# Where two input projections stand in a two-layer decoder step: at the gate and in the router instead of ahead of the output projection

## The reference

```python
for i in range(DEPTH):                                   # DEPTH = 2
    mix, nb, ns = mixer(rms_norm(x, norm_mix_g[i]), ...) # ends in m @ w_o
    x = x + mix
    hn = rms_norm(x, norm_ffn_g[i])
    if i % 2 == 0: f = swiglu(hn, w_dense_gu, w_dense_down)      # layer 0
    else:          f = moe(hn, w_router, w_gu, w_down)           # layer 1
    x = x + f
    gate = jax.nn.sigmoid(rms_norm(x, norm_ple_g[i]) @ w_ple_gate[i])
    x = x + gate * (p[i] @ w_ple[i])                     # the layer-input projection

def moe(h, ...):                                         # 8 experts, 2 per token
    logits = h @ w_router
    top_v, top_i = lax.top_k(logits, 2)
    top_w = jax.nn.softmax(top_v, axis=-1)
    ...
```

## Time and profile before

| | |
|---|---|
| median of three runs | 1804.52 us (1803.7 to 1807.8) |
| the profiled execution's own time | 1805.45 us |
| its span, first to last instruction | 1803.7 us |
| TensorE busy | 1756.8 us, 97% |
| VectorE / ScalarE / GpSimd busy | 1431.7 / 1079.1 / 151.7 us |
| mean granted TensorE clock | 0.99 of 2.4 GHz |

### The profile page before, as it was taken

One profiled execution on the slowest core, in us unless ns is written; L12 is line 12 of the kernel. 1 busy time (PEld: TensorE's weight loads), 2 busy tenths in 40 slices (PEclk: granted clock), 3 DMA queues, 4 the chain that ended last, 5 costly groups with the idle time before them and its releaser, 6 DMA issues.

```text
span 1803.7 us, 27952 instructions
## 1 busy us (share of the span) xinstructions
PE 1756.8 (97%) x10593; PEld 1562.5 (87%) x10593; DVE 1431.7 (79%) x1326; ACT 1079.1 (60%) x894; POOL 151.7 (8%) x158
## 2 busy tenths in 40 slices
PE   7999999999989999899999999999999999999996
PEld 6999999999989999788888888888888888888876
DVE  5875676566678766598898998998988989889886
ACT  4335544334443455476777777776777777777763
POOL 2112210000331113100000000000000000000003
PEclk9999999999999999899999999999999999999999
DMA  9754555655555545299999999999999999999970
GB/s 270 243 179 155 172 175 166 194 177 166 186 186 169 174 155 169 89 367 376 328 360 342 357 356 335 363 365 330 357 361 339 355 364 336 362 343 347 366 271 25
DMA packets 278010, 483.74 MB, mean 268 GB/s; under 512 B 7918, under 2 KB 126910, under 8 KB 277938
## 3 DMA queue, kind: packets, MB, share of 16 engines
q1 hardware_dynamic: 274734, 472.67, 75.3%
q0 software_dynamic: 2992, 9.92, 2.0%
q10 hardware_dynamic: 212, 0.14, 0.0%
HBM read 476.83 MB, written 5.87 MB: 268 GB/s over the span
## 4 chain that ended last, share of the span: by engine, by line
PE 90%; DVE 4%; DMA 2%; ACT 2%; issue 1%; POOL 0%; SPq 0%; DVEq 0%; POOLq 0%; ACTq 0%
PE PS L1656 11%; PE PS L1660 11%; PE PS L1659 11%; PE PS L1845 10%; PE PS L1848 10%; PE PS L1849 10%; PE PS L1676 6%; PE PS L1679 6%; PE PS L1680 6%; DMA raw<-in_w_in 2%; DVE wlo L1319 2%; PE PS L1636 1%; ACT whi L834 1%; PE PS L1694 1%; PE PS L2050 1%
## 5 line engine op out<-in xcount | busy, mean ns | idle before, releaser
L1319 DVE TENSOR_TENSOR wlo<-raw,whi 128x2048 fp32r<-128x2048 f32 x450 | 1036.9, 2307 | 241.9 <-ACT whi L834 237.6
L834 ACT ACTIVATE whi<-raw 128x2048 fp32r<-128x2048 f32 x450 | 862.3, 1918 | 393.4 <-PE PS L1845 166.9
L1656 PE MATMUL PS<-whi,xh 128*128 128x512 f32 x896 | 353.5, 395 | 1.0 <-DVE wlo L1319 0.9
L1660 PE MATMUL PS<-whi,xl 128*128 128x512 f32 x896 | 350.2, 391 | 0.0
L1659 PE MATMUL PS<-wlo,xh 128*128 128x512 f32 x896 | 349.4, 390 | 0.0
L1845 PE MATMUL PS<-xh,whi 128*128 128x264 f32 x1184 | 341.3, 288 | 6.2 <-DVE pg__51 L1361 3.8
L1848 PE MATMUL PS<-xl,whi 128*128 128x264 f32 x1184 | 337.9, 285 | 0.0
L1849 PE MATMUL PS<-xh,wlo 128*128 128x264 f32 x1184 | 337.8, 285 | 0.0
L1845 PEld LDWEIGHTS PS<-xh,whi 128*128 128x128 f32 x1184 | 225.5, 190 | 7.3 <-issue 4.0
L1848 PEld LDWEIGHTS PS<-xl,whi 128*128 128x128 f32 x1184 | 225.5, 190 | 0.2
L1849 PEld LDWEIGHTS PS<-xh,wlo 128*128 128x128 f32 x1184 | 224.3, 189 | 0.0
(11 more groups left out here) (291 smaller groups left out, 1841.9 us busy)
## 6 DMA issues: line engine op xcount, KB each, us to landing
raw<-in_w_exp_gu SPq DMA_DIRECT2D x224, 1024.0 KB, 5.8
raw<-in_w_exp_down SPq DMA_DIRECT2D x112, 1024.0 KB, 5.6
raw<-in_w_in SPq DMA_DIRECT2D x44, 1024.0 KB, 5.2
raw<-in_w_dense_gu SPq DMA_DIRECT2D x28, 1024.0 KB, 5.0
raw<-in_w_dense_down SPq DMA_DIRECT2D x16, 896.0 KB, 5.1
raw<-in_w_o SPq DMA_DIRECT2D x8, 1024.0 KB, 4.9
raw<-in_w_ple_gate SPq DMA_DIRECT2D x8, 1024.0 KB, 6.0
scr<-in_state_ret POOLq DMA_DIRECT2D x8, 512.0 KB, 4.8
```

The source lines that it names most:

```text
L834: nc.scalar.activation(whi[:, c % CAST, :], raw[:, c % RAW, :], ACT.Copy).then_inc(hi_done, 1)
L1319: v.tensor_tensor(wlo[:, c % CAST, :], raw[:, c % RAW, :], whi[:, c % CAST, :].bitcast(F32), ALU.subtract).then_inc(lo_done, 1)
L1656: ins = mm(PS[:, bank, :], gh[:, 128 * kk:128 * kk + 128], wh, start=kk == 0, stop=False)
L1660: ins = mm(PS[:, bank, :], gl[:, 128 * kk:128 * kk + 128], wh, start=False, stop=kk == 7)
```

## The change

Four things are changed together.

1. `pw` leaves its place between `ret` and `o` in both layers; `o` now starts with `chunk_late`, on the operands of `m_lo`.
2. In layer 0, `pw` stands between the down-projection and the gate, with the norm's sum of squares behind its tile 4. ScalarE copies tiles 0 to 4, takes the root, copies 5 to 7; VectorE makes the reciprocal first and then casts gate chunks 1 and 2.
3. In layer 1, `pw` stands in the router, tile by tile: tile 0 ahead of everything, 1 and 2 around the logits, 3 ahead of the ranks, 4 ahead of the gather, 5 between gather and turning, 6 and 7 behind the turning. It uses two of the ring's banks. The token groups are reordered, the low ones in three banks. The router weights are split in layer 1's `o` loop.
4. Experts are picked on the logits as they come, without the token's norm factor, which is positive and so changes no order; the factor is multiplied into the difference of the two picked logits before the exponential. Root, reciprocal and Newton step come behind the selection. The counts go to bank 7 and are ready together with the ranks; the gating block comes behind the copy of the first gather.

The core of the diff:

```diff
-        for name, n in (("in", 14), ("conv", 2), ("gate", 8), ("ret", 2), ("pw", 1), ("o", 4)):
+        order = [("in", 14), ("conv", 2), ("gate", 8), ("ret", 2), ("o", 4)]
+        order += [("ffn", 44), ("pw", 1), ("pg", 4)] if l == 0 else [("pw", 1), ("ffn", 0), ("pg", 4)]
+        for name, n in order:
...
@@ the mixer's end, TensorE
-                pw_pe(chunk, l)
-                for i in range(4):
-                    chunk(b["o"] + i, t["o"] + 2 * i, 8, 2, frt[:, 8:16, :], frt[:, 16:24, :],
-                          each=(m_lo, [8 * l + k + 1 for k in range(8)]) if i == 0 else None)
+                chunk_late(b["o"], t["o"], (m_lo, [8 * l + k + 1 for k in range(8)]), None, frt[:, 8:16, :], frt[:, 16:24, :])
+                for i in range(1, 4):
+                    chunk(b["o"] + i, t["o"] + 2 * i, 8, 2, frt[:, 8:16, :], frt[:, 16:24, :])
...
+                    pw_pe(chunk, l)
                     ple_pe(pe, chunk, stat, 0)
...
-            chunk(b["pw"], t["pw"], 2, 8, ph[:, 2 * l:2 * l + 2, :], pl[:, 2 * l:2 * l + 2, :])
+            chunk(b["pw"], t["pw"], 2, 8, ph[:, 2 * l:2 * l + 2, :], pl[:, 2 * l:2 * l + 2, :], norm=2, at_tile=4)
@@ layer 0's gate, ScalarE
                     dense_act(act, cast, root, split_x)
+                    act.wait_ge(tile_taken, t["pw"])
+                    for j in range(5):
+                        take_pw(j)
+                    root(NORM_OF["ple", 0])
+                    for j in range(5, KT):
+                        take_pw(j)
+                    cast(b["pw"] + AHEAD)
                     ple_act(act, cast, root, split_x, 0)
@@ layer 0's gate, VectorE
                     dense_dve(dve, v, cast, recip, take, split_x)
+                    recip(NORM_OF["ple", 0])
+                    cast(b["pw"] + AHEAD)
+                    dve.wait_ge(tile_taken, t["pg"])
                     ple_dve(dve, v, cast, recip, take, split_x, 0)
@@ the router, TensorE
+            def pw_tile(j):
+                if j == 0:
+                    ready(PWC)
+                pe.wait_ge(tile_taken, PW1 - 2 + j if j < 2 else PW1 + j - 1)
+                for k in range(2):
+                    ...
+                ins.then_inc(tile_ready, 1)
...
+            pw_tile(0)
+            token_hi(0)
+            token_hi(1)
+            pe.wait_ge(xl_ready, 32 + 4)
+            token_lo(0)
+            token_lo(1)
+            token_lo(2)
+            pw_tile(1)
+            token_hi(2)
             pe.wait_ge(wr_lo, 1)
...
             ins.then_inc(lgT_ready, 1)
+            token_hi(3)
+            pw_tile(2)
             pe.wait_ge(lgT_done, 1)
...
+            token_lo(3)
+            token_lo(4)
+            token_hi(4)
+            token_hi(5)
+            token_lo(5)
+            pw_tile(3)
+            pe.wait_ge(route_act, 1)
+            pe.wait_ge(route_dve, 1)
...
+            ins.then_inc(rank_ready, 1)
+            pw_tile(4)
...
             gather(0)
+            pw_tile(5)
             turn_operands(0)
+            pw_tile(6)
+            pw_tile(7)
             pe.wait_ge(routed, 1)
@@ the router, VectorE
-            dve.wait_ge(route_act, 1)
-            v.memset(rg[:, :, 1:2], 0.0).then_inc(dve_chain, 1)
-            n_chain[0] += 1
-            link(v.tensor_scalar(rt[:, 232:235], PS[0:TT, 7, 24:27], 1.0 / D, EPS, ALU.mult, ALU.add))
-            link(v.reciprocal(rg[:, :, 0], rt[:, 0:3]))
-            newton(rg[:, :, 0], rt[:, 232:235])
...
-            link(v.tensor_tensor(lg, PS[0:TT, 7, 0:24].rearrange("p (t e) -> p t e", t=3),
-                                 rg[:, :, 0:1].to_broadcast([TT, 3, 8]), ALU.mult))
+            dve.wait_ge(logit_ready, 1)
+            v.tensor_copy(lg, PS[0:TT, 7, 0:24].rearrange("p (t e) -> p t e", t=3)).then_inc(lg_done, 1)
...
             select(slice(0, 1))
...
+            link(v.tensor_tensor(dif, top[:, :, 0:2], top[:, :, 0:1].to_broadcast([TT, 3, 2]), ALU.subtract))
+            v.tensor_tensor(dif, dif, rg[:, :, 0:1].to_broadcast([TT, 3, 2]), ALU.mult).then_inc(route_dve, 1)
...
+            gathered(0)
...
             turned(0)
+            cast(CB[1]["pw"] + AHEAD)
```

More of the change, by code:

```diff
@@ L128, in tile_bases @@
         s = {}
-        rows = [("in", 28), ("conv", 8), ("gate", 16), ("ret", 8), ("pw", 8), ("o", 8)]
+        rows = [("in", 28), ("conv", 8), ("gate", 16), ("ret", 8), ("o", 8)]
         if l == 0:
             rows += [("gu0", 28), ("down0", 8), ("gu1", 28), ("down1", 8)]
-        for name, n in rows + [("pg", 8)]:
+        for name, n in rows + [("pw", 8), ("pg", 8)]:
             s[name] = at
@@ L244, in program, with pw_bank @@
         PG_BANK = (0, 1, 2, 4, 5, 6, 1, 2)
+        PW1 = TB[1]["pw"]
+        PW_BANK = ((PW1 - 3) % RING, (PW1 - 2) % RING)
+        TOKL_BANK = (5, 6, (PW1 - 1) % RING)
+        TOKENS = [(t, h) for h in range(2) for t in range(3)]
+        def pw_bank(p):
+            return PW_BANK[(p - PW1) % 2] if PW1 <= p < PW1 + 8 else p % RING
         def bank_of(p):
@@ L682, in ple_act @@
                     cast(b["pg"] + i + AHEAD, turns)
-                if i == 0:
+                if last and i == 0:
                     root(norm)
@@ L1276, in moe_dve @@
             last = most + 1
-            gathered(0)
             turned(0)
+            cast(CB[1]["pw"] + AHEAD)
             rescale(0)
@@ L1587, in moe_pe, with token, token_hi, token_lo @@
             b = CB[1]["ffn"]
+            PWC = CB[1]["pw"]
+            def pw_tile(j):
[3 more added lines that the diff above has]
+                for k in range(2):
+                    at = 1024 * k + 128 * j
+                    ins = three(PS[:, pw_bank(PW1 + j), 0:T], whi[:, PWC % CAST, at:at + 128],
+                                wlo[:, PWC % CAST, at:at + 128], ph[:, 2 + k, :], pl[:, 2 + k, :],
+                                k == 0, k == 1, j == 0 and k == 0)
+                ins.then_inc(tile_ready, 1)
+            def token(src, bank, n):
+                tile, h = TOKENS[n]
+                for k in range(4):
+                    ins = mm(PS[0:TT, bank, 128 * k:128 * k + 128],
+                             src[:, 4 * h + k, TT * tile:TT * tile + TT], idr[:, :], start=True, stop=True)
+                return ins
+            def token_hi(n):
+                if n > 1:
+                    pe.wait_ge(tokh_done, n - 1)
+                token(xht, 3 + n % 2, n).then_inc(tokh_ready, 1)
+            def token_lo(n):
+                if n > 2:
+                    pe.wait_ge(tokl_done, n - 2)
+                elif n == 2:
+                    pe.wait_ge(tile_taken, PW1)
+                token(xlt, TOKL_BANK[n % 3], n).then_inc(tokl_ready, 1)
+            pe.wait_ge(idr_done, 1)
+            pw_tile(0)
[7 more added lines that the diff above has]
+            token_hi(2)
             pe.wait_ge(wr_lo, 1)
-            pe.wait_ge(idr_done, 1)
             for k in range(KT):
@@ L1863, in chunk, with chunk_late @@
                     ins.then_inc(tile_ready, 1)
-                    if n == 0 and norm is not None:
+                    if n == at_tile and norm is not None:
                         stat(norm)
-            def chunk_late(c, p, each, norm):
+            def chunk_late(c, p, each, norm, ah, al):
                 ready(c)
```

180 lines of the change are left out of this document (92 added, 88 removed).

## The result

The changed kernel takes 1797.48 us (median of five runs, 1796.24 to 1797.69) against 1806.95 for the kernel before on the same chip (five runs, 1803.7 to 1807.8): ratio 0.995, 95% interval 0.9936 to 0.9964. It is faster by 0.5%. Forecast were 1793.0 with a range of 1786.5 to 1798.0: the time lies in it, 4.5 us above the number. It lies outside the forecast's own range, 1790.5 to 1796, without the rivals.

The account below looks back on a forecast made before the run. TensorE, busy 97% of the span, was taken as the bound. Terms -6.5 + 5.2 - 6.5 - 3.7 = -11.5 us from 1803.7 gave 1792.2, as median 1793.0; own range 1790.5 to 1796, with rivals (1), (2), (3), (5) 1786.5 to 1798.

Parts of the forecast that it names:

- A: Layer 0's mixer end: with the projection gone, the output projection starts earlier, at 205.19 instead of 211.71; gains 6.5 us.
- C: Layer 1's mixer end: the same as A, the output projection starting at 695.7 instead of 702.20; gains 6.5 us.
- B: Layer 0's gate: the added projection delays VectorE's row of work, so layer 1's first product comes later; costs 5.2 us.
- Rival (2): Layer 0's gate: its waits hide the projection, so B costs only 1.2 us; 1789.0 us in all; chance 0.06.
- Rival (3): Table loads: a drain starts each root or exponential 1.4 us later; +1.4 in B, +0.4 in router; 1794.8 us; chance 0.03.
- D: Router, last `o` to first expert product: shorter with projection tiles inside, clock falling again at the gather; gains 3.7 us.
- rival (1): Router: the clock holds through the gather, so D gives 7.3 us; 1789.4 us in all; chance 0.29.
- rival (5): Experts: they give part back through a late chunk 1 or 2, some 5 us; 1798 us; chance 0.07.
- Rival (4): Router: TensorE stays at 1.2 GHz from the first token groups on, D loses 7.7 us; 1804.4 to 1808.0; chance 0.03.

Follow-up runs that it names:

- gate_delay: `router_gl` with the reciprocal in layer 0's gate done four times, not once; one execution of 1802.1 us.
- cast_first: The changed kernel with one chunk of layer 0's gate weights cast ahead of the root and reciprocal; 1793.91 us, ratio 0.9927.
- scaled_first: The changed kernel with experts picked on the scaled logits again, behind root, reciprocal and Newton steps; 1800.12 us, ratio 0.9955.
- no_tiles: The changed kernel with layer 1's projection back ahead of `o`, the rest of the new router kept; 1803.52 us, ratio 0.9981.
- gl_early: The changed kernel with the split of the turned rows (`turned(0)`) ahead of VectorE's two `value_load`; 1796.42 us, ratio 0.9936.
- gate_only: The kernel before with layer 0's half alone: projection moved to the gate, `o` with `chunk_late`; 1806.95 us, ratio 0.9999.
- router_gl_again: `router_gl` run once more with identical code; 1795.42 us, ratio 0.9934.
- cast_gl: The changed kernel with the edits of `cast_first` and `gl_early` together; 1793.32 us, ratio 0.9929.
- router_gl: The changed kernel with layer 0 as before and `turned(0)` ahead of the two `value_load`; 1795.64 us, ratio 0.9936.

## Why the prediction was right and wrong

**A, right.** Forecast 6.5 us, measured 8.12 - 1.8 = 6.3, by the wait on the bank of `ret` tile 6 (1.64 us) and with no wait on an operand behind it. Up to the last take of `o` it is 5.9, as VectorE takes the last two tiles a little later behind their products. **C** is the same again, 6.3 and 5.8.

**B, right, and the main lesson.** Forecast 5.2 us. On the clock of the kernel before (3.55 us later) the reciprocal starts at 486.43 (forecast 486.3), the first gate take at 494.42 (494.3), layer 1's first product at 514.88 (514.8). B is 5.3 us, and the wait of 3.84 us is there with 3.85. Rival (2), that 4.6 us of waits hide 5.8 us of work, is refuted: VectorE ends these waits, so work put in front of them moves them. `gate_delay` shows it without any projection, and `cast_first`, with 1.8 us less ahead of the first take, makes B 1.1 us cheaper.

Rival (3) is refuted too: the table load of 481.07 with its 1.28 us ends at 482.35 and the root starts at 482.36. The Trainium skill (ScalarE: Activation LUTs, What ACT_TABLE_LOAD costs) adds a drain of about 1.38 us to a load of 1.28; this trace agrees with the load and shows no drain.

**D, mis-sized: the step that failed is the clock.** Forecast were 3.7 us, from "I take it that it falls again as the gather starts"; measured were 27.7 - 21.3 = 6.4. It was rival (1), with 0.29: the clock holds through the gather. (The base varies: from the second profile of the kernel before, 26.1 us, D is 4.7.) The stretch ahead of it came as forecast: I had "1.35 us of very small products, 0.7 us of projection and 0.9 us of nothing", and the trace has 1.4 us of ranks and counts, a tile, and 0.73 us of idle. What failed was the verdict on it, "closer to the stretch that fell (half busy) than to the one that held". TensorE had been busy without a break for 6 us ahead of the ranks. `scaled_first` has 1.76 us more of idle there and loses the clock, `no_tiles` loses it too (one profile each); all nine profiles with both the tiles and the unscaled choice keep it. Rival (1)'s 7.3 us were missed by 0.9, which is the size of the wait on the split behind two `value_load`. I had put 0.6 us for all short waits; without this one (`gl_early`) it is 20.5 us from the last `o` product to the first expert product, and rival (1) has 20.4.

**The sum.** A to D measured: -6.3 + 5.3 - 6.3 - 6.4 = -13.7 us, forecast -11.5. The profiled spans differ by 8.0 and the medians of the five runs by 9.5. In the spans the rest is +2.3 ahead of o0, +1.6 in layer 1's mixer, +1.3 at the end and 0.5 in small differences of takes. My sum held that these stretches move as they are. In the first and the last, the same code varies by 3.2 and 1.7 us between profiles, so the difference of one pair is not the change's. In the middle one it is not settled. The stretch of gate and mixer took 213.8 to 217.6 us in five profiles with the old gate (mean 215.5) and 222.2 to 223.1 in six with the new one (mean 222.8): 7.3 us apart, 5.3 of them B, 2 more by falls of the clock behind it. That fits falls that follow the new gate, and the median of `gate_only`, which gains nothing from 5.9 - 5.3. Of the eight profiles with the projection in the gate, seven have two falls in layer 1's retention, and of the six without it one has. But `router_gl_again` is that one, `cast_gl` (219.5) has one fall with the projection, and `gate_delay`, late without it, has one. The medians of the kernel before moved from 1804.52 (three runs) to 1806.4 to 1807.4 (10 to 21 runs) as well, so 2.4 us of the miss against 1793.0 are the base's: from 1806.95, -11.5 would have given 1795.5. So that the time lies in the range owes something to luck. D came out better than its term, the rest worse, and the range reached past 1796 only for rival (5), which did not come.

The Trainium skill (TensorE: Matmul & The Clock Gate, What's actually happening) says that the same kernel begins with a different number of slow products from one run to the next, by where the gate stands when the kernel starts. No run here shows the start; further on these traces show the like: layer 1's retention has one fall and none in two profiles of the kernel before, one and two in those of `router_gl`.

**Rivals (4) and (5)** did not come: the clock is 1.00 all through the router, and the experts' stretch is 1006.8 us before and after. Rival (4)'s sum had a slip that touches nothing else: 34.7 us against 27.7 is a loss of 7.0 in D and not of 7.7.

## What to carry to other kernels

Work moved into a wait is free only if the engine that ends the wait can start its own row of work as early as before: at the gate VectorE ended it, and 5.8 us of TensorE's work put ahead of it cost 5.3. In the router it was worth more than its length, since the waits were several and short and filling them kept TensorE at 2.4 GHz. Split such a change into its halves and time each: here one half made all of the gain that could be measured. And cut profiles into stretches before comparing positions: the same code moved by up to 3 us between profiles.

## What the runs showed of the hardware

- Two `value_load` on VectorE, behind a wait on its own semaphore and with nothing queued ahead, left it idle for 1.70 us; behind the split (1.29 us) only 0.55 us of them showed. Independent work belongs ahead of them.
- In this router, 0.73 us of idle and the ranks' and counts' very small products (18 rows in the trace) ahead of the gather did not cost the clock (nine profiles), and with 1.76 us more of idle it was lost (one profile). The gather then took 5.46 us and not 3.03.
- TensorE loses 1.7 us at a time to falls of the clock in stretches where its busy time is 10.00 of 10 us (0.83 in 150 to 160), not only where it waits. In the retention stages all 36 falls of the 14 profiles began between 0.2 us before and 1.4 us after the end of a block of eight one-column products (1.95 us); 76 of the 112 blocks had none, and what decides was not found.
